# Output projection of a two-layer trunk: second half as seven quarter products, its routing chain moved behind them, and a reordered end

## The reference

```python
for layer in range(2):
    hn = rmsnorm(h, attn_norm[layer])
    h = h + from_heads(o) @ w_out            # o: the mixer's heads, 512 x 1024; w_out 1024 x 1024
    t = rmsnorm(h, ffn_norm[layer])
    # top-1 group of 4, top-2 experts of 8 inside it, gates from the two softmaxes
    h = h + sum_over_experts(gate * (silu(t @ w_gate[e]) * (t @ w_up[e])) @ w_down[e])
return rmsnorm(h, final_norm)
```

## Time and profile before

| | us |
|---|---|
| median of three runs | 1024.78 |
| lowest and highest | 1023.83, 1028.85 |
| the profiled execution's own time | 1025.55 |
| its span, first to last instruction | 1023.7 |
| mean granted TensorE clock | 0.989 of full speed |
| PE busy | 965.0 (94%) |
| DVE busy | 458.7 (45%) |
| ACT busy | 238.7 (23%) |
| POOL busy | 184.5 (18%) |
| DMA | 275.73 MB, mean 269 GB/s |

### The profile page before, as it was taken

The page is one execution under the profiler, slowest core; times in us unless marked ns, Lnnn a source line. Parts: engine busy times, 40 slices in busy tenths (PEclk is TensorE's granted clock), DMA queues, the critical chain, the costliest instruction groups (busy, mean ns, idle before and its releaser), DMA issues.

```text
span 1023.7 us, 13907 instructions
## 1 busy us (share of the span) xinstructions
PE 965.0 (94%) x5576; PEld 652.2 (64%) x5576; DVE 458.7 (45%) x1158; ACT 238.7 (23%) x590; POOL 184.5 (18%) x136
## 2 busy tenths in 40 slices
PE   7999999999999899999899999999998999998986
PEld 6888688868556566665444877456755766665542
DVE  5644722386463332222236548677546232222215
ACT  3323700281221000000012226366121100000002
POOL 5540172006001111112103201002401011111100
PEclk9999999999999999999999999999999999999998
DMA  9649502154768999999989220145285999999996
GB/s 334 221 132 206 158 13 105 49 208 170 305 229 312 417 420 418 421 419 420 417 339 277 83 82 2 48 189 209 78 353 206 380 421 418 421 419 420 420 380 258
DMA packets 67026, 275.73 MB, mean 269 GB/s; under 512 B 16067, under 2 KB 20659, under 8 KB 42890
## 3 DMA queue, kind: packets, MB, share of 16 engines
q1 hardware_dynamic: 56960, 257.48, 65.2%
q0 software_dynamic: 10000, 17.34, 4.9%
HBM read 260.64 MB, written 30.44 MB: 284 GB/s over the span
## 4 chain that ended last, share of the span: by engine, by line
PE 72%; DMA 17%; DVE 4%; SPq 3%; issue 2%; POOL 1%; ACT 0%; DVEq 0%; POOLq 0%
PE bank L976 16%; PE bank L1248 12%; DMA K<-rows,small 9%; PE bank L1025 6%; PE bank L1089 6%; PE bank L1262 5%; DMA W<-in_moe_w_up 5%; PE bank L1098 5%; PE bank L1043 3%; PE bank L1059 3%; DMA hnT<-in_moe_w_down 3%; PE bank L1448 3%; SPq L515 2%; PE bank L1270 1%; PE bank L1159 1%
## 5 line engine op out<-in xcount | busy, mean ns | idle before, releaser
L2123 DVE SCALAR_TENSOR_TENSOR PT<-bank,small,PT 128x256 f32<-128x256 f32 x32 | 15.5, 484 | 206.1 <-PE bank L1248 206.1
L1262 PE MATMUL bank<-D,PT 128*64 128x512 f32 x416 | 101.6, 593 | 4.8 <-ACT PT L1696 2.6
L757 POOL DMA_INDIRECT expert_rows<-K,small x30 | 30.3, 1011 | 342.7 <-DVE K L2145 318.0
L1248 PE MATMUL bank<-W,PT 128*64 128x256 f32 x640 | 79.4, 390 | 9.6 <-DMA W<-in_moe_w_up 6.4
L2145 DVE SCALAR_TENSOR_TENSOR K<-K,small,bank 128x512 f32<-128x512 f32 x64 | 47.8, 747 | 86.4 <-PE bank L1262 86.2
L1248 PE MATMUL bank<-W,cst 128*64 128x256 f32 x640 | 78.1, 384 | 0.0
L1696 ACT ACTIVATE PT<-bank 128x256 f32<-128x256 f32 x32 | 12.3, 383 | 263.0 <-PE bank L1254 263.0
L1656 ACT ACTIVATE P<-P,nm 128x128 f32<-128x128 f32 (+5 forms) x128 | 68.3, 536 | 22.1 <-DVE nm L1902 21.6
L1025 PE MATMUL bank<-K,Q 128*128 128x256 f32 (+3 forms) x256 | 70.5, 417 | 1.4 <-DVE nm L1902 1.0
L1248 PEld LDWEIGHTS bank<-W,PT 128*64 128x64 f32 x640 | 50.2, 139 | 33.3 <-issue 10.9
L1262 PEld LDWEIGHTS bank<-D,PT 128*64 128x64 f32 x416 | 36.0, 137 | 48.9 <-issue 43.7
(11 more groups left out here) (314 smaller groups left out, 1804.7 us busy)
## 6 DMA issues: line engine op xcount, KB each, us to landing
D<-in_moe_w_down SPq DMA_DIRECT2D x48, 1024.0 KB, 19.2
W<-in_moe_w_gate SPq DMA_DIRECT2D x40, 1024.0 KB
W<-in_moe_w_up SPq DMA_DIRECT2D x36, 1024.0 KB, 19.4
hnT<-in_moe_w_down SPq DMA_DIRECT2D x12, 1024.0 KB, 17.4
W<-in_e_w_in SPq DMA_DIRECT2D x5, 2048.0 KB
expert_rows<-K SPq DMA_DIRECT2D x2, 4096.0 KB, 35.8
V<-in_moe_w_gate SPq DMA_DIRECT2D x6, 1024.0 KB
Q<-in_moe_w_gate SPq DMA_DIRECT2D x6, 1024.0 KB
```

What stands on the lines that cost most here:

```text
L1248: last = nc.tensor.matmul(bank[b][at, 0:256], XT[k // 4][:, k % 4, at], w[:, 256 * k:256 * k + 256], start=(k == 0), stop=(k == KD - 1))
L1262: last = nc.tensor.matmul(bank[5 + half][at, :], hT[:, 128 * c + 64 * a:128 * c + 64 * a + 64], d[:, col:col + 512], start=(c == 0), stop= ...
```

## The change

There are two parts.

**Second half of the projection, both layers.** The second half is now made like the first, by seven quarter products (56 matmuls of 256 columns for 32 of 512). It reuses the row sums T1 to T4; POOL makes the weight sums after those of the first half; ACT copies four parts out and DVE adds the parts in a new order. The last two products are cut by chunk (`chunk_product`), the first pair of products runs ahead of all routing, and most of the routing stands behind the products. ACT copies both halves of the transposed rows. On SP, the five downs no longer follow the first half: they wait for the last product, since D0 to D4 hold sums and parts until then.

**End, second layer.** Each identity product stands right behind its own late product, and the last chunk is normed and written in two halves.

```diff
-                sp.wait_ge(s_og, 11 * lay + 7)
+                sp.wait_ge(s_og, 15 * lay + 7)
                 load_gate_up(lay, 4)
-                sp.wait_ge(s_oga, 8 * lay + 4)
-                for e in (0, 1, 2, 6, 3):
-                    load_down(lay, e)
                 rows = h_dram[lay]
...
-                sp.wait_ge(s_og, 11 * lay + 11)
+                sp.wait_ge(s_og, 15 * lay + 15)
+                for e in (0, 1, 2, 3):
+                    load_down(lay, e)
                 load_half(lay, 5, 1)
+                load_down(lay, 6)
...
+                pool.wait_ge(*landed("K", ("out", 2 * lay + 1)))
+                a11, a12, a21, a22 = second_weights()
+                s1, s2, s4 = second_S
+                pool.wait_ge(s_og, 15 * lay + 3)
+                nc.gpsimd.tensor_tensor(s1, a21, a22, ALU.add).then_inc(s_wsum, 1)
+                pool.wait_ge(s_og, 15 * lay + 4)
+                pool.wait_ge(s_wsum, before + 5)
+                nc.gpsimd.tensor_tensor(s2, s1, a11, ALU.subtract).then_inc(s_wsum, 1)
+                nc.gpsimd.tensor_tensor(a21, a11, a21, ALU.subtract).then_inc(s_wsum, 1)
+                pool.wait_ge(s_wsum, before + 6)
+                nc.gpsimd.tensor_tensor(s4, a12, s2, ALU.subtract).then_inc(s_wsum, 1)
...
                 first_features()
-                for half, buf in ((1, "K"),):
-                    pe.wait_ge(*landed(buf, ("out", 2 * lay + half)))
-                    for c in range(C):
-                        product(half, c, 0, 1)
...
+                quarter_product(bank[0], a11, b11, True)
+                quarter_product(bank[1], a12, b21, True)
+                pe.wait_ge(s_oga, 8 * lay + 4)
+                first_half(0)
+                pe.wait_ge(s_opart, parts + 1)
+                pe.wait_ge(s_wsum, sums + 2)
+                quarter_product(bank[0], s2, t2, False)
+                pe.wait_ge(s_opart, parts)
+                logits(0, 0)
+                quarter_product(bank[2], a22, t4, True)
+                pe.wait_ge(s_opart, parts + 2)
+                pe.wait_ge(s_wsum, sums + 3)
+                quarter_product(bank[0], a21, t3, False)
+                chunk_product(bank[7], s1, t1, 0, True)
+                second_half(0)
+                chunk_product(bank[0], s1, t1, 1, True).then_inc(s_og, 1)
+                logits(0, 1)
+                first_half(1)
+                second_half(1)
+                pe.wait_ge(s_opart, parts + 4)
+                pe.wait_ge(s_wsum, sums + 4)
+                chunk_product(bank[7], s4, b22, 0, False).then_inc(s_og, 1)
+                logits(1, 0)
+                logits(1, 1)
+                first_half(2)
+                chunk_product(bank[0], s4, b22, 1, False).then_inc(s_og, 1)
+                ranks(0)
+                logits(2, 0)
+                second_half(2)
+                stay_busy(1, 512)
+                logits(2, 1)
+                first_half(3)
                 second_half(3)
+                stay_busy(1, 512)
+                logits(3, 0)
+                logits(3, 1)
+                slots(0)
+                ranks(1)
+                stay_busy(3, 512)
                 slots(1)
                 ranks(2)
-                logits(3, 1)
-                stay_busy(2, 512)
+                stay_busy(3, 512)
                 slots(2)
                 ranks(3)
                 stay_busy(1, 256)
...
+                then(add_part(0, 0, 2, 0))
+                add_bank(1, 9, 0, 2, 0)
+                then(add_part(1, 2, 4, 0))
+                then(add_bank(2, 11, 0, 2, 1))
+                for c in range(2):
+                    add_part(2, c, c + 1, 1, 256 * c).then_inc(s_oga, 1)
+                then(add_part(2, 2, 4, 1))
+                root_inverse(2 * lay + 1, 0)
+                choose(0)
+                then(add_part(3, 2, 4, 1))
+                add_bank(7, 14, 2, 3, 0).then_inc(s_oga, 1)
+                root_inverse(2 * lay + 1, 1)
+                choose(1)
+                add_bank(0, 15, 3, 4, 0, 256).then_inc(s_oga, 1)
+                place(0)
+                root_inverse(2 * lay + 1, 2)
+                choose(2)
+                place(1)
+                root_inverse(2 * lay + 1, 3)
+                choose(3)
+                place(2)
+                place(3)
...
                 for c in range(C):
                     last = late_product(lay, c)
-                    if c not in summed[lay]:
-                        last.then_inc(s_late, 1)
-                for c in summed[lay]:
-                    pe.wait_ge(s_yld[c], 32 * (lay + 1))
...
+                    if c in summed[lay]:
+                        pe.wait_ge(s_yld[c], 32 * (lay + 1))
...
-                    norm_chunk(4, 3)
+                    root_inverse(4, 3)
+                    for half in range(2):
+                        part = slice(512 * half, 512 * half + 512)
+                        nc.vector.scalar_tensor_tensor(hn_row[:, 3, part], h[:, 3, part], rstd[:, 3:4], gain[:, part],
+                                                       ALU.mult, ALU.mult).then_inc(s_hn, 1)
```

144 lines of the change are left out of this document (71 added, 73 removed).

## The result

| | median, us | runs | lowest to highest |
|---|---|---|---|
| before | 1024.86 | 6 | 1022.46 to 1028.85 |
| after | 1036.84 | 6 | 1031.95 to 1038.71 |

The ratio is 1.0112, with a 95% interval of 1.0092 to 1.0131: the changed kernel is 12 us slower. Forecast were 1028.3 us and a range of 1020 to 1036; the result lies just above it. The profiled execution of after took 1037.79 us with a span of 1035.9; that of before 1025.55 with 1023.7, so the two traces differ by 12.2 us.

The account below looks back on a forecast made before the run. DMA, full while the experts run, was taken as the bound, so DMA time lost before that moves the end: +4.4 us over two layers, -0.9 at the end, +3.5 in sum, from 1024.78 to 1028.3 us; range 1020 to 1036.

Parts of the forecast that it names:

- What bounds the kernel: Experts' stage: DMA is full at 418 GB/s, so only DMA time lost before saturation moves the end.
- Second half on TensorE, POOL and ACT: Projection's second half: 3.5 us less a layer on TensorE, 0.8 arriving at the last slots; POOL and ACT hide, cost 0.
- The rival by which the projection's length decides: Stream has slack and the experts' start counts: -3.5 us a layer and -0.9, 1016.9 us; chance 0.14.
- The ledger of lost time: DMA idle from expert 4's load to saturation: 21.0 to 22.5 us lost against 20.3; taken as +2.2 a layer.
- three gathers 1.5 MB: Ledger entry for DMA before the first gates end: three gathers of 0.5 MB each, read by 55.9 us.
- The clock: TensorE idle 4 to 5 us before the first gates; the lower clock then costs 0 to 1.5 us.
- The end: Second layer's reordered identity products, last chunk normed and written in halves: -0.9 us, bounds -0.3 and -1.3.
- The caught gather: First gather stuck in the load backlog, 11.6 us, loads start at 64.4: +6.4 us a layer, 1036.7 us; chance 0.16.
- The slipping gather: First gather waits for only one 1 MB load, 6.1 us: -0.7 to -0.2 us a layer, 1023.0 us; chance 0.24.

Follow-up runs that it names:

- delayed gates: The kernel before with ten instead of four throwaway products of 512 columns ahead of the first transposes, all loads unchanged; measured 1034.4 us, ratio 1.0101.

## Why the prediction missed

**What bounds the kernel: right.** The experts' windows hold 418 to 420 GB/s in every kernel looked at, and the end follows the loss. It is not exact: summed over the layers, after lost 9.3 us more than before and took 12.2 more in the trace. 0.9 of the rest lies ahead of the second half. 1.8 lie behind the last loads of layer 1: from the last down's issue to the experts' rows it was 23.1 us, 21.3 before. There an idle stretch lies ahead of down products at a lower clock:

```profile
997.94 5.35 PE L1297 MATMUL bank<-D,PT 128*64 128x512 f32 x16 [2.76 <-DMA D<-in_moe_w_down]
...
997.00:1002.00 5.00, 4.06 (x12) 1.61 (x14) 0.75 (x1) 0.00 (x0) 0.00 (x0) 0.66 1.02 412
```

In before the same group took 3.65 us. Over all kernels and both layers this tail varies between 18.8 and 23.9 us, with no order that I can see by the change; what sets it stays open.

**Second half on TensorE, POOL and ACT: right.** Last slots were forecast at 44.4; they start at 305.27, 43.7 after the start in this trace, and the gather is issued 1.4 us earlier than before, for 0.8 forecast. POOL's sums are done at 258.7 and its small loads at 263; nobody waits. The rival by which the projection's length decides had its condition met (slots earlier) and its result missing.

**The ledger of lost time: the step that failed.** Up to the gates its entries for after are good. Lost by 282.2 us are 15.3 us for 15.8 (108 GB/s from 261.6 on; DMA went idle at 271 instead of 267, behind 187 GB/s from 262 to 267), from there to 300 us 4.4 for 3.8 (316 GB/s). Stores and downs go out within 0.7 us, the gather takes 8.06 us for 8.3, and the release is at 59.9 and 59.2 where the gates were to end at 58.7 to 60.2. What failed is how this was turned into a loss against before: "21.0 to 22.5 against 20.3". The first is a computed loss, the second the *measured* loss of before. By the same ledger, release + 0.9 - 38.9 us for the prefetch, after has 21.9 and 21.2, as forecast, but before has 16.9 and 17.6. The measured losses exceed it by 3.6 and 3.4 us in before and by 4.1 and 3.6 in after, in both kernels alike; the prediction gave 0 to 1.5 us for that, and to after alone. What should have been subtracted is release from release. Forecast that way it is +3.8 to +5.3 a layer (58.7 to 60.2 against 54.9) and 1031.5 to 1034.5 us; measured are +4.9 and +3.6, instead of the +2.2 and +2.2 taken. The terms are all in the table: gather issued 1.4 earlier; its wait 8.1 and 7.9 instead of 3.7 and 4.1; from the rows to the release 7.2 and 6.4 instead of 5.3 and 5.2.

About half of the excess is a term of the ledger that was mis-sized: "three gathers 1.5 MB", 15.5 MB in all, 16.3 in the rates' unit. POOL's queue moved, for all 32 gathers and 30 scatters and some small loads:

```profile
q0 software_dynamic: 10000, 17.34, 4.7%
```

That is at most 0.28 MB each. The windows from the first gate load to 0.9 us behind the release agree: they hold 15.4 MB in before and 15.6 in after, 0.8 less than counted, or 1.9 us that were booked as transfer and were idle. So at the gates 4.2 us were lost from 314 to 323 us where 1.4 to 2.9 were booked (1.2 to 2.7 by the prediction's own times, 0.9 behind 58.7 to 60.2 against 58.4). The other half is a stream below its full rate in stretches in which the queue isn't empty.

That the stretch behind the release is slow on both sides is measured: in before 315 to 335 us ran at 367 GB/s, in after 325 to 345 at 374, and with delayed gates 321 to 341 at 365; the rows, before and delayed gates:

```profile
315.00:335.00 20.00, 19.60 (x157) 13.66 (x155) 5.44 (x12) 3.00 (x5) 0.00 (x0) 1.00 0.93 367
```

```profile
321.00:341.00 20.00, 19.60 (x158) 13.72 (x156) 5.70 (x14) 3.01 (x5) 0.09 (x1) 1.00 0.94 365
```

**The clock: at the upper edge of what was taken.** Taken were 0 to 1.5 us, from an average over 5 us in the experts. It cost 1.9 in layer 0 and 1.2 in layer 1, since transposes and half of the gates' products all lay behind the idle stretch; the runs with more throwaway products gave it back.

**The end: mechanism there, worth nothing.** Forecast -0.9, bounds -0.3 and -1.3; measured 0 (ratio 1.0006 in before; 1036.74 against 1036.84 in after). Chunk 2's rows came about as forecast: its identity product began 5.6 us behind the first add (1023.26 against 1017.68), where 1010.8 is 5.4 behind 1005.40. The step that failed is the time of the products: from there to the end of chunk 3's identity product it was 5.4 us for 5.15. So chunk 3's add came 0.2 later instead of 0.2 earlier. The halved last chunk gave 0.3 us from that add to the end of the span (7.1 for 7.4), where 0.7 was forecast.

**The rivals.** The caught gather's time, 1036.7, is the measured one by luck: the gather stood behind the backlog, but took 8.06 us, not 11.6, and the loads started at about 60, not at 64.4. The slipping gather is out: nothing of the gather's own queue lay ahead of it, and it took 8.06. In the 8 us from 306 to 314 the DMA moved 424 GB/s and then fell to 284, so the rows landed about when the backlog was through: 13.8 MB had moved by then, and the last half load and two gathers were left. The Trainium skill ("DMA: Bandwidth & Descriptors", section "Queues, rings and completion order") has each DMA engine take turns between the queue rows with work. By that the gather should have been served beside the loads; the trace does not agree, and no run here shows why.

## What to carry over

Moving a prefetch behind a product doesn't just shift bytes: it puts them in front of the next small, dependent transfer, and what that one releases. If a model reproduces a kernel's measured idle time only up to a remainder, apply it to both kernels and take the difference, never the model of one against the measurement of the other. Take a gather's bytes from what its queue moved, not from the size of its buffer. A saturated stream has two limits, when its next loads are released and how much of the prefetch is then unread; test each with the other held fixed before counting a gain.

## What the runs showed of the hardware

- **A gather into a buffer of 512 KB, about half of it moved, behind a backlog:** 3.4 to 3.8 us to TensorE's start beside a nearly empty queue (4.1 and 4.2 where TensorE was still busy), 4.3 to 4.8 with the last loads held but some still under way, 7.3 to 8.6 behind the downs, on another queue than theirs.
- **TensorE's clock after a short wait:** the level had fallen behind idle stretches of 2.0 to 5.6 us ahead of the transposes and in one case of 1.39 (the gates' first 16 matmuls in 2.5 to 3.7 us for 1.95), and it had not behind eight stretches of 0.2 to 1.0 us, in six traces. That one stretch does not tell it all: in the second layer of before the eight throwaway products took 5.26 us for 3.68, at a granted 0.67 from 783 to 788 us, with waits of 1.36 and 0.40 us ahead of them. The fall need not come with the first instruction behind the wait: behind 2.07 us idle the transposes still ran in 1.16 and the gates after them in 3.61; behind 1.99, in the other layer, it was 1.97 and 2.68.
- **A full share is not a full rate:** after has stretches at a share of 1.01 and 341 GB/s behind the first gates, and 420 at the same share in the experts:

```profile
330.00:335.00 5.00, 5.00 (x49) 4.00 (x47) 0.00 (x0) 0.47 (x1) 0.00 (x0) 1.00 1.01 341
```

What makes the same share move less there wasn't tried.
